# A hybrid attention and mixture-of-experts layer on one core: the third head of the cross-attention output product goes from split to plain fp32, and one piece of expert 1's weights is loaded in three parts at other places of the queue

## What is computed

```
x += concat([sliding_window_attention, multiscale_pool]) @ W_out
h  = rmsnorm(x)
q  = rmsnorm((h @ xq_w) in 4 heads of 128);  k, v = split(rmsnorm(mem) @ xkv_w), k normed per head
x += softmax(q k^T / sqrt(128)) v @ xo_w          # memory cross attention, xo_w is 512 x 2048
h  = rmsnorm(x)
x += sum over a token's 2 chosen experts: gate * ((silu(h @ w_gate[e]) * (h @ w_up[e])) @ w_down[e])
```

## Time and profile before

| | |
|---|---|
| median of three executions | 1669.48 us (1668.78 to 1670.71) |
| the profiled execution: its own time, its span | 1669.28 us, 1667.5 us |
| TensorE busy | 1553.3 us, 93% of the span |
| VectorE, ScalarE, GpSimd busy | 638.5, 357.6, 165.4 us |
| bytes moved by DMA | 484.47 MB, mean 291 GB/s |
| mean granted TensorE clock | 0.986 of full speed |

### The profile page before, as it was taken

One profiled execution on the slowest core, in us unless ns is written; L12 is line 12 of the kernel. 1 busy time (PEld: TensorE's weight loads), 2 busy tenths in 40 slices (PEclk: granted clock), 3 DMA queues, 4 the chain that ended last, 5 costly groups with the idle time before them and its releaser, 6 DMA issues.

```text
span 1667.5 us, 18188 instructions
## 1 busy us (share of the span) xinstructions
PE 1553.3 (93%) x7236; PEld 891.7 (53%) x7236; DVE 638.5 (38%) x774; ACT 357.6 (21%) x639; POOL 165.4 (10%) x235
## 2 busy tenths in 40 slices
PE   8999999999999999799999899889889899899997
PEld 7788776768887567634343333434334434334343
DVE  6655656652223433513232322323323323313324
ACT  6422334342222244211110110011011011101011
POOL 4570054510000000100000000000000000000000
PEclk9999999999999999999999999999999999999999
DMA  8333322353215031799999999999999999999997
GB/s 304 102 101 85 91 65 63 122 164 101 100 52 202 1 127 47 315 384 430 410 425 429 428 428 428 428 421 414 429 420 420 425 419 428 428 428 423 428 422 284
DMA packets 90238, 484.47 MB, mean 291 GB/s; under 512 B 6067, under 2 KB 44109, under 8 KB 62157
## 3 DMA queue, kind: packets, MB, share of 16 engines
q1 hardware_dynamic: 86696, 470.84, 69.8%
q0 software_dynamic: 3392, 12.92, 2.3%
q10 hardware_dynamic: 100, 0.03, 0.0%
HBM read 484.81 MB, written 8.39 MB: 296 GB/s over the span
## 4 chain that ended last, share of the span: by engine, by line
PE 68%; DMA 17%; DVE 8%; ACT 3%; issue 2%; SPq 1%; POOL 0%; DVEq 0%; POOLq 0%; ACTq 0%
PE ps L2233 23%; DMA weight_ring<-in_expert_w_up_dram 15%; PE ps L1940 10%; PE ps L1814 8%; PE ps L2259 8%; PE ps L2194 5%; PE ps L1993 3%; DVE residual L1619 3%; ACT weight_ring L888 1%; PE ps L1776 1%; PE ps L2322 1%; PE ps L2057 1%; DMA residual<-in_x_dram 1%; DVE weight_ring L1291 1%; PE ps L2082 1%
## 5 line engine op out<-in xcount | busy, mean ns | idle before, releaser
L2233 PE MATMUL ps<-weight_ring,transposed_acts 128*64 128x512 f32 x2000 | 467.4, 608 | 41.1 <-DMA weight_ring<-in_expert_w_up_dram 40.3
L2233 PEld LDWEIGHTS ps<-weight_ring,transposed_acts 128*64 128x64 f32 x2000 | 166.9, 140 | 334.2 <-issue 262.0
L1619 DVE TENSOR_TENSOR residual<-ps,residual 128x1024 f32<-128x1024 f32 x128 | 150.9, 1220 | 250.1 <-PE ps L2194 249.3
L2259 PE MATMUL ps<-weight_ring,transposed_acts 128*64 128x512 f32 x960 | 214.2, 599 | 17.8 <-DVE transposed_acts L1629 17.8
L1635 DVE SCALAR_TENSOR_TENSOR y_low<-ps,proj_buffer,y_high 64x1024 fp32r<-64x1024 f32 x60 | 77.0, 1283 | 199.5 <-ACT y_high L1080 198.5
L2259 PEld LDWEIGHTS ps<-weight_ring,transposed_acts 128*64 128x64 f32 x960 | 67.6, 138 | 146.8 <-issue 142.8
L1080 ACT ACTIVATE y_high<-ps,proj_buffer 64x1024 fp32r<-64x1024 f32 x60 | 66.5, 1109 | 288.1 <-PE ps L2259 287.4
L1069 ACT ACTIVATE transposed_acts<-ps 128x512 f32<-128x512 f32 x32 | 19.1, 597 | 465.0 <-PE ps L2233 465.0
L1814 PE MATMUL ps<-mix_high,w_in_high 128*128 128x512 f32 x288 | 117.4, 408 | 1.4 <-issue 1.4
L1814 PE MATMUL ps<-mix_high,w_in_low 128*128 128x512 f32 x288 | 112.4, 390 | 0.0
L1814 PE MATMUL ps<-normed_low,w_in_high 128*128 128x512 f32 x288 | 112.4, 390 | 0.0
(11 more groups left out here) (323 smaller groups left out, 1891.1 us busy)
## 6 DMA issues: line engine op xcount, KB each, us to landing
weight_ring<-in_expert_w_down_dram SPq DMA_DIRECT2D x63, 2048.0 KB, 15.1
weight_ring<-in_expert_w_gate_dram SPq DMA_DIRECT2D x61, 2048.0 KB, 16.3
weight_ring<-in_expert_w_up_dram SPq DMA_DIRECT2D x60, 2048.0 KB, 20.5
weight_ring<-in_w_in_dram SPq DMA_DIRECT2D x18, 1024.0 KB, 5.6
weight_ring<-in_w_out_dram SPq DMA_DIRECT2D x16, 1024.0 KB, 5.0
weight_ring<-in_xkv_w_dram SPq DMA_DIRECT2D x8, 1024.0 KB, 7.2
residual<-in_x_dram SPq DMA_DIRECT2D x8, 1024.0 KB, 12.3
weight_ring<-in_xq_w_dram SPq DMA_DIRECT2D x4, 1024.0 KB, 9.8
```

Of the source, the lines that this page charges most:

```text
L1619: v.tensor_tensor(part, ps[:, bank:bank + 2, :].rearrange("p b n -> p (b n)"), part, ALU.add).then_inc(signal, 1)
L2233: ins = mm(ps[side * SLOTS:(side + 1) * SLOTS, 0, :], xsT[:, k, par * SLOTS:(par + 1) * SLOTS], gate_up_weights(e, u, kk), start=(k == 0), ...
L2259: ins = mm(ps[half, 4 + n % 2, :], act_t[:, f * SLOTS:(f + 1) * SLOTS], w[:, n * 512:(n + 1) * 512], start=(f == 0), stop=(f == KF - 1), s ...
```

## The change

`CUT` becomes 2: head 2 of the output product is no longer split, and goes through one plain fp32 matmul like head 3. Slot 6 is then not needed by cross attention, and unit 3 of expert 1 (slots 6 and 7; it is the second half of w_up) is loaded in three parts: the first 2048 columns right behind xo_w, the next 1536 columns when the last tile's attention output has been copied out, and the last 512, the region of `junk`, at the old place. The unit's count of landings goes from one to three.

```diff
-        CUT = 3
-        xo_hi = [att_lo[:, :, :].rearrange("p k s -> p (k s)")[:, 0:CHK], att_lo[:, :, :].rearrange("p k s -> p (k s)")[:, CHK:2 * CHK],
-                 w_hi[:, :, :, :].rearrange("p r k n -> p (r k n)")[:, 0:CHK]]
-        xo_lo = [w_lo[:, :, :, :].rearrange("p r k n -> p (r k n)")[:, c * CHK:(c + 1) * CHK] for c in range(2)] + [top[:, 0, :]]
+        CUT = 2
+        xo_hi = [att_lo[:, :, :].rearrange("p k s -> p (k s)")[:, 0:CHK], att_lo[:, :, :].rearrange("p k s -> p (k s)")[:, CHK:2 * CHK]]
+        xo_lo = [w_lo[:, :, :, :].rearrange("p r k n -> p (r k n)")[:, c * CHK:(c + 1) * CHK] for c in range(2)]
...
+            sp.dma_start(unit(3)[:, 0:CHK], expert_unit(1, 3)[:, 0:CHK]).then_inc(landed[unit_slot(3)], 16)
             for u in (1, 2, 0, 3, 4, 5):
+                if u == 3:
+                    part = slice(2 * CHK - 512, 2 * CHK)
+                    sp.dma_start(unit(u)[:, part], expert_unit(1, u)[:, part]).then_inc(landed[unit_slot(u)], 16)
+                    continue
                 if u == 1:
                     sp.wait_ge(used, SEQ_XQ + 2)
                 if u == 2:
                     sp.wait_ge(xq_done, NT)
                 if u == 0:
+                    sp.wait_ge(oT_ready, NT)
+                    part = slice(CHK, 2 * CHK - 512)
+                    sp.dma_start(unit(3)[:, part], expert_unit(1, 3)[:, part]).then_inc(landed[unit_slot(3)], 16)
                     sp.wait_ge(o_done, 28)
                     sp.wait_ge(parts_done, 32)
-                sp.dma_start(unit(u), expert_unit(1 if u == 3 else 0, u)).then_inc(landed[unit_slot(u)], 16)
+                sp.dma_start(unit(u), expert_unit(0, u)).then_inc(landed[unit_slot(u)], 16)
...
-                    if t == 0 and n == 0:
-                        chunk_landed(pe, SEQ_XO + CUT)
-                    ins = mm(ps[:, n % 2, :], H[:, CUT, part], slot(8 + CUT)[:, cols], start=False, stop=True)
+                    for c in range(CUT, XH):
+                        if t == 0 and n == 0:
+                            chunk_landed(pe, SEQ_XO + c)
+                        ins = mm(ps[:, n % 2, :], H[:, c, part], slot(8 + c)[:, cols], start=False, stop=(c == XH - 1))
                     ins.then_inc(o_done, 1)
...
                     if u == 3:
-                        loads -= 1
+                        loads += 1
```

## The result

The kernel after took 1673.43 us (median of 20 runs, 1671.20 to 1675.23), the kernel before 1670.57 us beside it (20 runs). The ratio is 1.0018, 95% interval 1.0012 to 1.0024: slower by 2.0 to 4.0 us, where +2.0 was predicted. That +2.0 stands against the lower edge of the interval; the two medians are 2.9 us apart. The profiled execution of after took 1675.23 us, its span 1673.5. It is the longest of the 20, so its differences from before add up to more than the median's.

The account below looks back on a forecast made before the run. The load queue paces the kernel after 861 us, but TensorE's clock sets it back at 734 and 806; +2.6 us of arithmetic less 0.6 of gather gives +2.0, 1671.4 us, range 1667.5 to 1673.6.

Parts of the forecast that it names:

- the rival with the low clock: One more low-clock stretch before 806 us, 1.5 us on top of the forecast: +3.5 us, 1673.0; chance 0.14.
- Three rounded matmuls for one pair, +2.6 us: In cross attention's output product, each of 16 groups gets 0.16 us longer, all on the path: +2.6 us.
- The gather, -0.6 us of 0 to -4.5: At 699 us, the gather's 8.72 us shrink because the load queue beside it is lighter: -0.6 us taken.
- The free parts: Dropped head 2 splitting, smaller tile copies, and the unit's first 1 MB and middle 0.79 MB: each taken as zero.
- The dry stretch at 733 grows to 3 to 5 us: The DMA engines' idle stretch at 733 us would grow from 1.6 to 3 to 5 us.
- the gather fell under 7 us: Sign of being wrong: the gather, expected at 7.2 to 8.7 us, takes less than 7.
- waits for weights shrank after 861: Sign of being wrong: TensorE's waits for weights after 861 us get shorter.
- w_down of expert 1 leaves as late as TensorE is: SP issues this load, at 734.17 us in before, as late as TensorE is; everything after shifts by 2 us.
- TensorE does not wait for weights before 861: Between 708 and 861 us TensorE waits for DMA once, for the gather (4.9 us), and never for weights.
- The sum: Whole kernel: +2.6 for the groups and -0.6 for the gather make +2.0 us, 1671.4 us predicted.
- the queue keeps its 4.3 us: Rival: the load queue bounds from 676 us on and its 4.3 us are kept: -1.7 us, 1667.8; chance 0.10.
- the gather finds free engines: Rival: the gather lands in 4.2 us: -1.9 us, 1667.6, chance 0.07; with full clock too -3.4, 1666.1, chance 0.04.

Follow-up runs that it names:

- after_swap: The changed kernel with DVE doing the whole first router turn ahead of the second tile's row scale; 1.0005 (0.9995 to 1.0015) of the kernel before.
- loads_only: Kernel before with the change's loads; head 2's product left out, three rounded matmuls on head 1's operands in its place; 0.9971 (0.9961 to 0.9981).
- loads_twice: loads_only with the whole unit 3 of expert 1 loaded again at its old place in the queue; 0.9974 (0.9966 to 0.9983) of the kernel before.
- after_late: The changed kernel with the extra expert's second and third MB sent behind the gather and first up unit; 1.0023 (1.0014 to 1.0032) of the kernel before.
- before_swap_late: before_swap with the extra expert's second and third MB sent behind the gather; 0.9987 (0.9978 to 0.9995) of the kernel before, 1668.59 us.
- head2_out: Kernel before with all its loads; head 2's three rounded matmuls use head 1's operands, so head 2's product is left out; 0.9978 (0.9969 to 0.9986).
- math_double: Kernel before with heads 1 and 2 both unrounded (`CUT = 1`), loads as before; 1.0055 (1.0041 to 1.0069), +9.2 us.
- math_only: Kernel before with the change's arithmetic alone (head 2 in plain fp32), loads as before; 1.0034 (1.0021 to 1.0048), +5.7 us.
- before_swap: Kernel before with DVE doing the whole first router turn ahead of the second tile's row scale; 0.9987 (0.9978 to 0.9995), 1668.59 us.
- before_again: The kernel before, unchanged, run once more for a second profile; 0.9998 (0.9989 to 1.0006) of the kernel before.

## Why the prediction was right, and where it was short

The change costs what was forecast to within its scatter, +2.0 predicted and 3.0 us (2.0 to 4.0) measured, and the largest term was right. In part it is luck: one term was missing (+1.7 us) and another was too small by 0.8 us the other way. The measured median of 1673.43 us lies 0.2 us below the upper end of the range, 1673.6, and nearer to the price of the rival with the low clock, 1673.0, than to the forecast of 1671.4; 1.1 us of that is the kernel before, which took 1670.57 beside it for the 1669.48 that the forecast started from.

**Three rounded matmuls for one pair, +2.6 us: right.** 3.11 us between groups for a predicted 3.10, 3.26 with two pairs. No other engine covers any of it: the gather's start moves by 4.4 and 8.8 us, of which the groups are 2.6 and 5.2.

**The clock in cross attention, taken as nothing: this is the term that was missing.** It is worth +1.7 us. The mechanism stood among the rivals ("one more stretch at the low clock"), with a chance of 0.14 and a price of 1.5 us for the stretch, but I had looked for it around the gather, where the row of 0.86 was the earlier trace rows. It came at 643, ahead of the gather. And it isn't chance: all six profiles with head 2 unrounded and DVE's order as it was have 6.8 us of low clock there, all five with TensorE's instructions as before have 3.4. The Trainium skill (TensorE: Matmul & The Clock Gate, What's actually happening) says that the place of the change varies between runs of one kernel; the low stretches between 683 and 731 do so here, in place and in length. At 643 the place varies a little (the product ahead takes 2.72 us in one profile of after and 3.40 in the other), the length doesn't. What doubles it was not separated. TensorE's wait at 640 isn't it: without the wait both kernels lose 3.4 us of low clock, and after_swap keeps its 3.4 us more. In after the stretch takes in part of the router's product and a group of `cross_out`, in before little but the group.

**The gather, -0.6 us of 0 to -4.5: right in sign and bounds, mis-sized.** It takes 7.3 us in the profile of after and 7.3 in after_swap, with the loads of before 8.4 to 9.2 in six profiles. That is -1.4 against the one of before, and near the -1.5 that I had worked out for 1.3 MB still queued; I had taken 1.8 MB and a queue that lasts until 0.2 us before the gather's transfer ends, but the engines' share is 0.60 in the third microsecond before it lands, 0.35 in the second and 0.07 in the last. In loads_only it takes 8.0, in loads_twice 8.4. Where 13.6 us of low clock after 683 have delayed it further it takes 4.3 and 4.4, and 4.4 in after_late, where nothing is queued. before_swap_late, with full engines for the first 3.5 us only, lies between with 6.5. The Trainium skill (DMA: Bandwidth & Descriptors, Queues, rings and completion order) has the engines take turns between queues with work; the lengths of 7.3 to 9.2 with a queue beside and 4.3 to 4.4 without agree, though they would fit other ways of sharing as well.

**The free parts: right as far as they can be seen.** The chain of after shows no row of ACT or DVE that is longer, the rows from 521 to 562 us keep their 0.23, and the 1 MB behind xo_w and the middle piece leave at 528.79 and 644.16 with nothing waiting for them. They were not tried one by one.

**"The dry stretch at 733 grows to 3 to 5 us": wrong.** It shrank, from 1.5 us to 0.7 at 737. The queue ran out earlier, at 708 to 712, while SP waits for the gather in front of the first up unit, and it starts again only when the gather has landed. The share from 708 to 712 is 0.26, so 3.0 us are idle, for 0.6 in before (0.85). From the issue of unit 0 to w_down of expert 1 the engines are idle for some 4.0 us in after (a share of 0.93 over 57.1 us) and 1.8 in before (0.97 over 58.5), and that stretch is 1.4 us shorter: together 3.6 of the 4.3 us that the queue had less. I had followed the queue from the gather to 733 and passed over this wait. The conclusion stays: the gain in the queue is lost, and after 861 the load queue moves as much as before.

**By its own signs.** The prediction called itself wrong if the dry stretch didn't grow, and it didn't; if the gather fell under 7 us, and it took 7.3 in the first profile of after but 4.3 in the second; and if waits for weights shrank after 861, and they didn't (40.3 us in before, 44.7 and 43.7 in after). The gather and the last piece of the unit leave 4.4 and 4.2 us late, not 2.6; w_down of expert 1 leaves as late as TensorE is, as forecast.

**"TensorE does not wait for weights before 861": true of before, but with no room.** There the unit in question was issued at 751.69 and landed 16.7 us later, 0.1 us before TensorE came to it. In after TensorE is idle for it for 2.10 and 0.26 us, and the block gets 3.0 and 1.15 us longer. The wait isn't peculiar to the change: it is there without the moved load in head2_out (1.3), math_double (1.3), math_only (0.4) and before_swap (1.4), and no such row stands in before_again, loads_only, loads_twice and after_swap. What decides when it comes was not separated. In after the unit is issued at 754.84 in both profiles, 2.9 and 3.6 us late, and takes 19.7 and 17.9 us to land for 16.7. The prediction had taken it as nothing.

**The sum.** Against the kernel before: +2.6 for the groups, +1.7 for the clock and -1.4 for the gather are +2.9 us. The end of block 0's down product is 2.9 us late in the profile, and there the sum ends. Behind it comes the wait for weights, 3.0 us, and 2.9 + 3.0 = 5.9 is the profile's whole difference (its span is 6.0 us longer, 5.8 once the 0.23 are off). The second profile has 3.6 + 1.15 = 4.7 for 4.4 us. The measured difference is 1.0018, 3.0 us (2.0 to 4.0). That it equals the sum without the wait proves nothing to a tenth: both profiles have some of the wait, and how much a usual execution has isn't known.

**The rivals.** That the queue keeps its 4.3 us is refuted by the result and by head2_out beside loads_only. That the gather finds free engines happens in the second profile of after, but it doesn't bring the faster kernel that I had priced, since after_late has it too. The rival of the clock happened, 60 us ahead of where I had looked for it.

**What stays open.** Whether moving the load is worth anything by itself. math_only and after, 1.0034 (1.0021 to 1.0048) and 1.0019 (1.0009 to 1.0030), say 2.5 us with intervals that overlap; loads_only and head2_out say 1 us or nothing. What doubles the low stretch at 643. And why the experts' stretch runs at 426 for 423 GB/s with head 2's product left out.

## What to carry to other kernels

A term of arithmetic that is on the path can be read to a hundredth of a microsecond from the distance of two groups, but a longer run of matmuls can also change how long the low clock lasts near it: cut the trace of before finely around the changed part, find the low stretches there, and price a longer one, as well as at the places where the mean clock of a wide stretch shows it. A wait of TensorE can cost more than the idle time shown for it (3.0 us for 2.1 here): compare the length of the whole block. When a queue gets lighter, follow it to the next instruction at which its issuer waits for something else; the gain ends there. And an experiment that leaves a product out changes the data of everything behind it: it needs a control with the same product left out and nothing else, or it tells a story of its own.

## What the runs showed of the hardware that I had not expected

- Where the clock falls within the second half of the router's product (16 matmuls with 36 columns, 2.72 us in after, 2.72 to 3.50 in six profiles) it stays low for 6.8 us; where it falls at their end (1.98 us in before, 1.97 to 2.20 in five profiles) for 3.4.
- A TensorE wait of 2.10 us made a row of 64 matmuls 2.99 us longer, one of 0.26 us made it 1.15 longer: 0.89 us on top both times.
- An indirect gather of 1 MB takes 4.3 to 4.4 us with free engines in three kernels, and 7.3 to 9.2 us with a queue beside it in ten.
- The rate of the loads from 1000 to 1400 us is 426 to 427 GB/s in the three kernels with head 2's product left out and 423 to 424 in the eleven others, worth some 3 us; head2_out has the same instructions as before, so the data are what differs.
